# Attention inside a decoder block: two heads' gathers on the two halves of the array's columns, and the running product scanned in place in SBUF

## The reference

```python
def block(args):
    qi, i = args
    logits = jnp.einsum('bqhd,bkhd->bhqk', qi, k, preferred_element_type=jnp.float32) * scale
    mask = key_pos[None, :] < q_pos[:, None]
    log_beta = jax.nn.log_sigmoid(logits)
    log_1m_beta = jnp.where(mask, jax.nn.log_sigmoid(-logits), 0.0)
    after = lax.cumsum(log_1m_beta, axis=3, reverse=True) - log_1m_beta
    w = jnp.where(mask, jnp.exp(log_beta + after), 0.0)
    return jnp.einsum('bhqk,bkhd->bqhd', w.astype(v.dtype), v)
```

## Time and profile before

| | us |
|---|---|
| three runs: median | 2991.63 |
| lowest, highest | 2988.93, 2992.62 |
| the profiled execution: span from its first to its last instruction | 2988.6 |

### The profile page before, as it was taken

How to read it: one execution, slowest core, us unless ns; L and a number is a source line. 1 busy time by engine, 2 the same in 40 slices (tenths; PEclk the granted TensorE clock), 3 DMA queues, 4 the chain that set the end, 5 groups by cost and what they waited for, 6 DMA issues and landing times. The chain is left out here.

```text
span 2988.6 us, 43206 instructions
## 1 busy us (share of the span) xinstructions
PE 2801.2 (94%) x14883; PEld 2366.7 (79%) x14883; DVE 1855.9 (62%) x2803; ACT 1357.4 (45%) x2268; POOL 906.7 (30%) x711
## 2 busy tenths in 40 slices
PE   6999977889999998997899899999999899999998
PEld 5888854779889897885788778887888787878787
DVE  5334348867778786555567675657555748484753
ACT  4222225667767675222344455555555424242421
POOL 0111101645555551310000022223333344434442
PEclk9999988989999999998999999999999999999999
DMA  5433344282322203443123334333544364656554
GB/s 171 104 87 82 98 128 58 71 216 54 71 57 58 61 22 103 136 145 134 57 99 106 120 103 141 110 112 116 182 140 137 103 168 101 170 103 158 113 113 85
DMA packets 291396, 328.21 MB, mean 110 GB/s; under 512 B 114072, under 2 KB 220576, under 8 KB 290976
## 3 DMA queue, kind: packets, MB, share of 16 engines
q1 hardware_dynamic: 276960, 291.96, 32.9%
q0 software_dynamic: 13824, 33.56, 7.5%
q10 hardware_dynamic: 464, 0.79, 0.1%
HBM read 206.57 MB, written 126.88 MB: 112 GB/s over the span
## 5 line engine op out<-in xcount | busy, mean ns | idle before, releaser
L3260 PE MATMUL f_ps_bank<-f_big,h_wv 128*128 128x512 f32 x1280 | 502.6, 393 | 25.3 <-DVE f_big L3106 18.6
L3262 PE MATMUL f_ps_bank<-f_big,h_wv 128*128 128x512 f32 x1280 | 500.1, 391 | 0.0
L3261 PE MATMUL f_ps_bank<-f_big,h_wv 128*128 128x512 f32 x1280 | 500.0, 391 | 0.0
L738 POOL TENSOR_TENSOR a_w<-a_on,a_left 128x640 f32<-128x640 f32 (+5 forms) x192 | 282.4, 1471 | 244.7 <-DVE a_left L790 113.1
L3003 ACT ACTIVATE h_wv<-h_w_sum 128x512 fp32r<-128x512 f32 x252 | 159.0, 631 | 351.1 <-PE f_ps_bank L3262 348.8
L2946 POOL TENSOR_TENSOR h_w_sum<-h_w_raw 128x512 f32<-128x512 f32 x63 | 90.6, 1438 | 730.3 <-DMA h_w_raw<-in_w_up 452.1
L3260 PEld LDWEIGHTS f_ps_bank<-f_big,h_wv 128*128 128x128 f32 x1280 | 241.4, 189 | 82.4 <-issue 27.2
L3262 PEld LDWEIGHTS f_ps_bank<-f_big,h_wv 128*128 128x128 f32 x1280 | 241.4, 189 | 50.6
L3261 PEld LDWEIGHTS f_ps_bank<-f_big,h_wv 128*128 128x128 f32 x1280 | 241.6, 189 | 49.5
L880 PE MATMUL a_ps_y<-a_wt,a_v 128*96 128x128 f32 x2176 | 269.9, 273 | 3.6 <-DVE a_yt L813 2.1
L3102 DVE TENSOR_TENSOR h_wv<-h_w_raw,h_wv 128x512 fp32r<-128x512 f32 x189 | 171.5, 908 | 155.0 <-ACT h_wv L3003 151.6
(11 more groups left out here) (402 smaller groups left out, 6155.7 us busy)
## 6 DMA issues: line engine op xcount, KB each, us to landing
h_w_raw<-in_w_up SPq DMA_DIRECT2D x32, 1024.0 KB, 6.6
a<-h_xr SPq DMA_DIRECT2D x128, 256.0 KB, 3.4
h_w_raw<-a SPq DMA_DIRECT2D x32, 1024.0 KB, 5.2
h_raw<-in_w_down SPq DMA_DIRECT2D x32, 512.0 KB, 6.6
out<-h_xr POOLq DMA_DIRECT2D x64, 256.0 KB, 4.7
out<-h_xr POOLq DMA_DIRECT2D x32, 512.0 KB, 5.6
p_xt<-in_x SPq DMA_DIRECT2D x16, 512.0 KB, 4.5
q<-p_raw SPq DMA_DIRECT2D x64, 128.0 KB, 2.5
```

The lines of the kernel that those rows point to most:

```text
L738: pool.tensor_tensor(w[m % WS][:, 0:k1 - k0], on[m % ONS][:, 0:k1 - k0], left[a][i % 2][:, at + k0 + 1:at + k1 + 1], ALU.mult).then_inc(we ...
L3260: pe.matmul(o, wv(i, 0)[:, k, :], hv(i, 0)[:, k, :], start=(k == 0), stop=False)
L3261: pe.matmul(o, wv(i, 0)[:, k, :], hv(i, 1)[:, k, :], start=False, stop=False)
L3262: mm = pe.matmul(o, wv(i, 1)[:, k, :], hv(i, 0)[:, k, :], start=False, stop=(k == KH - 1))
```

## The change

Two things are changed, both in `stick_breaking`.

The gathers of the two heads of a unit are issued together, tile by tile in turn, head 0 into rows 0 to 63 of the output and head 1 into rows 64 to 127, with 64 columns of v each. A pair is gathered after both its slots, in every second iteration. One semaphore counts pairs. y of both heads is then in one tile, and is copied by one DVE instruction and stored by one DMA.

The second sigmoid is written to `left` in SBUF, and the scan runs over `left` in place. The wait for `left` moves from DVE to ACT, and `score(m)` waits for the second sigmoid of slot m - 2, no more for its scan.

```diff
-        yt = [sb(f"yt{a}", [HEAD, 2, BANK]) for a in range(2)]
+        yt = sb("yt", [P, 2, BANK])
...
+        def wait_gathered(eng, slots):
+            wait(eng, pairs_gathered, (slots + 1) // 2)
...
-                act.activation(z, z, ACT.Sigmoid, scale=-SCALE).then_inc(sig_off, 1)
+                at = SEQ - (i + 1) * P
+                if blocks_of[m] >= 2:
+                    act.wait_ge(weighed, final_slot[blocks_of[m] - 2] + 1)
+                act.activation(left[a][i % 2][:, at + k0:at + k1], z, ACT.Sigmoid, scale=-SCALE).then_inc(sig_off, 1)
...
                 dve.wait_ge(sig_off, m + 1)
-                if blocks_of[m] >= 2:
-
-                    dve.wait_ge(weighed, final_slot[blocks_of[m] - 2] + 1)
                 if not first:
                     dve.wait_ge(scanned, m - 1)
-                dve.tensor_tensor_scan(left[a][i % 2][:, at + k0:at + k1][:, ::-1], z_ps[m % 2][:, 0:k1 - k0][:, ::-1],
+                part = left[a][i % 2][:, at + k0:at + k1][:, ::-1]
+                dve.tensor_tensor_scan(part, part,
                                        one[:, 0:1].to_broadcast([P, k1 - k0]),
...
-                if last:
+                if last and a == 1:
                     part = s * 4 + i // 4
-                    dve.wait_ge(gathered, m + 1)
-                    if part >= 2:
-                        dve.wait_ge(y_stored[part % 2], part // 2 * 2 * DMA)
-                    dve.tensor_copy(yt[a][:, part % 2, i % 4 * P:(i % 4 + 1) * P], y_ps[a][0:HEAD, 0:P]).then_inc(y_copied, 1)
+                    wait_gathered(dve, m + 1)
+                    wait(dve, y_stored[part % 2], part // 2 * DMA)
+                    dve.tensor_copy(yt[:, part % 2, i % 4 * P:(i % 4 + 1) * P], y_ps[blocks_of[m] % 2][:, 0:P]
+                                    ).then_inc(y_copied, 1)
...
                 if m >= 2:
-                    pe.wait_ge(scanned, m - 1)
+                    pe.wait_ge(sig_off, m - 1)
...
-                    cols = slice(row * HEAD, row * HEAD + TALL)
-                    mm = pe.matmul(y_ps[a][0:TALL, 0:P], v[a][(2 * s + half) % 3][:, cols],
-                                   wt[m % WTS][:, t, :], start=(first and t == 0), stop=(last and t == tiles - 1))
-                mm.then_inc(gathered, 1)
+                    cols = slice(row * HEAD, (row + 1) * HEAD)
+                    for a in range(2):
+                        mm = pe.matmul(y_ps[blocks_of[m] % 2][a * HEAD:(a + 1) * HEAD, 0:P], v[a][(2 * s + half) % 3][:, cols],
+                                       wt[(m + a) % WTS][:, t, :], start=(first and t == 0), stop=(last and t == tiles - 1))
+                mm.then_inc(pairs_gathered, 1)
...
-                if m >= GATHER_LAG:
-                    gather(m - GATHER_LAG)
+                if m > GATHER_LAG and m % 2:
+                    gather(m - GATHER_LAG - 1)
```

More of the change, by code:

```diff
@@ L591, in stick_breaking @@
     WIDE = 1024
-    TALL = 3 * HEAD // 2
     UNITS = attention_units()
@@ L607, in stick_breaking @@
         k2_lo = [[sb(f"k2_lo{a}{r}", [P, HALF], F32R) for r in range(3)] for a in range(2)]
-        v = [[sb(f"v{a}{r}", [P, BLOCKS * HEAD // 2 + HEAD // 2]) for r in range(3)] for a in range(2)]
+        v = [[sb(f"v{a}{r}", [P, BLOCKS * HEAD // 2]) for r in range(3)] for a in range(2)]
         ident = sb("ident", [P, P])
@@ L637, in stick_breaking @@
         copied_d = sem("copied_d")
-        gathered = sem("gathered")
+        pairs_gathered = sem("pairs_gathered")
         y_copied = sem("y_copied")
@@ L684, in load_half @@
                                          k_dram[2 * s + a, part * HEAD:(part + 1) * HEAD, cols]).then_inc(k_loaded[half], DMA)
-                wait(sp, gathered, (step_out + 1) * PER_STEP)
+                wait_gathered(sp, (step_out + 1) * PER_STEP)
                 for a in range(2):
                     h = 2 * s + a
-                    sp.dma_start(v[a][r][:, 0:BLOCKS * HEAD // 2].rearrange("p (i d) -> p i d", d=HEAD),
+                    sp.dma_start(v[a][r][:, :].rearrange("p (i d) -> p i d", d=HEAD),
                                  v_dram[cols, h * HEAD:(h + 1) * HEAD].rearrange("(i p) d -> p i d", p=P)).then_inc(v_loaded[half], DMA)
@@ L692, in store_half @@
                 for part in (2 * half, 2 * half + 1):
[L693 to L697, removed]
+                    wait(sp, y_copied, s * BLOCKS + (part + 1) * 4)
+                    sp.dma_start(yt_dram[s * P:(s + 1) * P, part * BANK:(part + 1) * BANK], yt[:, part % 2, :]
+                                 ).then_inc(y_stored[part % 2], DMA)
             load_begin(sp, 0, slice(0, BANK), begin_loaded[0], begin_loaded[0])
             for a in range(2):
-                sp.dma_start(v[a][0][:, 0:BLOCKS * HEAD // 2].rearrange("p (i d) -> p i d", d=HEAD),
+                sp.dma_start(v[a][0][:, :].rearrange("p (i d) -> p i d", d=HEAD),
                              v_dram[0:HALF, a * HEAD:(a + 1) * HEAD].rearrange("(i p) d -> p i d", p=P)
@@ L713, in _ @@
                 else:
-                    sp.wait_ge(y_stored[0], (2 * s + 1) * 2 * DMA)
+                    sp.wait_ge(y_stored[0], (2 * s + 1) * DMA)
                     ahead.load_ys(sp, yt_dram, ahead_loaded)
@@ L718, in _ @@
             for part in range(2):
-                sp.wait_ge(y_stored[part], 2 * STEPS * 2 * DMA)
+                sp.wait_ge(y_stored[part], 2 * STEPS * DMA)
         @block.gpsimd
@@ L758, in copies @@
                         act.wait_ge(turned, g + 1)
-                        if m >= WTS:
-                            act.wait_ge(gathered, m - WTS + 1)
+                        wait_gathered(act, m - WTS + 1)
                         act.activation(wt[m % WTS][:, t0:t0 + n, :], wt_ps[g % 2][:, 0:n * P].rearrange("p (t q) -> p t q", q=P),
@@ L775, in _ @@
             dve.memset(one[:, :], 1.0).then_inc(ones_ready, 1)
[L776 to L779, removed]
+            dve.wait_ge(ones_ready, 5)
             def scan(m):
@@ L799, in copies @@
                         dve.wait_ge(turned, g + 1)
-                        if m >= WTS:
-                            dve.wait_ge(gathered, m - WTS + 1)
+                        wait_gathered(dve, m - WTS + 1)
                         dve.tensor_copy(wt[m % WTS][:, t0:t0 + n, :],
@@ L825, in _ @@
             pe.wait_ge(constants, 5)
-            pe.wait_ge(ones_ready, 11)
             def score(m):
@@ L867, in gather @@
             def gather(m):
-                s, a, i, k0, k1, first, last = SLOTS[m]
-                wait_copied(pe, first_group[m + 1] - 1)
+                s, _, i, k0, k1, first, last = SLOTS[m]
+                wait_copied(pe, first_group[m + 2] - 1)
                 if first:
@@ L873, in gather @@
                         pe.wait_ge(v_loaded[i // (BLOCKS // 2)], (s + 1) * 2 * DMA)
-                    wait(pe, y_copied, 2 * (blocks_of[m] - 1) + a + 1)
+                    wait(pe, y_copied, blocks_of[m] - 1)
                 tiles = (k1 - k0) // P
```

## The result

The changed kernel took 3031.78 us (median of four runs, 3029.23 to 3033.84), the kernel before 2990.28 (2985.85 to 2992.62): ratio 1.0138, 95% interval 1.0124 to 1.0153. Slower by 41 us; 3031 was forecast, range 3011 to 3078.

The account below looks back on a forecast made before the run. PE bounded attention before; now scans and products in turns would: 552 + 7 + 4 = 563 us, plus 4.5 us behind, ending at 1177.5 instead of 1137.66, so 2991.6 + 40 = 3031 us, range 3011 to 3078.

Parts of the forecast that it names:

- The exclusion: In attention, a scan with two SBUF inputs and GpSimd's product cannot overlap; chance 0.78, 3031 us, 3011 to 3078.
- The sum: Attention's scans and products in turns: 552 us lower bound, plus 7 and 4, gives 563 us.
- the queue: Scans and products each waiting behind the other, saving 0.14 us each; five slots in six, the others costing 7 us.
- short slots: Slots starting each of attention's four steps, bound by latency: 4 us added.
- The upper bound: Each product starts 0.08 us after its scan, and the next scan waits for that product: 594 us.
- The tail: From attention's last product to its end: transposes, copies, the last pair's gathers, a copy of y; 4.5 us.
- The gathers: Attention's paired gathers overlap in the array's halves: PE saves 119 us, shape changes add 19, load 416 us.
- Rival 1: Scans and products in attention overlap as before and the array's halves overlap: 2910 us, chance 0.10.
- Rival 2: In attention, scans and products overlap as before but the array's halves don't: 2991 to 3011, say 3002 us, chance 0.04.
- Rival 3: Exclusion, with PE also bounding attention through serial or dearer halves or a falling clock: 3080 to 3100 us, chance 0.08.
- The sigmoid into SBUF: Attention's second sigmoid written to SBUF costs ScalarE 1 us, nothing; z comes free about 1.7 us sooner.
- Copies of y: VectorE loses 64 of attention's 128 copies of y, 17 us less load; the rest fit into GpSimd's turns.

Follow-up runs that it names:

- experiment 1: Kernel before with only the second sigmoid written to left in SBUF and the scan in place there; gathers unchanged: 3041.71 us, ratio 1.0171.
- experiment 5: Changed kernel with the scan's column of ones in a PSUM bank, y in one bank and copied one slot earlier: 2953.41 us, ratio 0.987.
- Experiment 3: Changed kernel with z in PSUM as the scan's ignored second operand, scores waiting for the scan again: 2952.66 us, ratio 0.9875.
- Experiment 10: Changed kernel with each pair's gather cut into two shares, after the odd and the next even slot: 3021.49 us, ratio 1.0102.
- Experiment 4: Changed kernel with VectorE waiting for product m - 1 before scan m: 3123.61 us, ratio 1.0446.
- Experiment 6: Experiment 2 with all of head 0's blocks in a pair first, then all of head 1's: 3029.19 us, ratio 1.0126.
- experiment 7: Kernel before with gathers of 64 columns of v instead of 96, still one head at a time: 3044.81 us, ratio 1.018.
- experiment 2: Changed kernel with the second sigmoid back in PSUM, the scan reading it there, and the waits of before: 2954.97 us, ratio 0.988.
- Experiment 8: Experiment 2 with each pair's gather cut into two shares, a fifth wt buffer, y copied one slot later: 2938.78 us, ratio 0.983.

## Why the prediction was right, and where its steps were off

**The exclusion (right, shown).** Two SBUF inputs, though one is a single repeated column, make scan and product take turns: experiment 1 gets all of the loss without the pairs, and experiment 5 removes it by moving only that column to PSUM (its other edits, one bank for y and an earlier copy of y, touch neither the scan nor the product). Experiment 3 removes it with z in the column's place. The rule that the prediction took from the Trainium skill (SBUF — State Buffer, § SBUF: two separate sides) holds for this operand too; 2.29 became up to 4.02 us.

**The sum (right in size, partly by luck).** From the first scan at 610.55 to the last product's end at 1173.43 it is 562.9 us; 563 were forecast as 552, plus 7 for one slot in six out of the queue, plus 4 for short slots. Two terms were off, in opposite directions. The queue saves more than was taken: a waiting scan saves its 0.14 us (2.29 - 2.14 = 0.15 above), but a waiting product 0.20, not 0.14. With that the bound for a queue that never runs dry is 605.7 - 192 x 0.34 = 540 us, an estimate from these rows, and not 552. Experiment 10 bears this out: it reaches 552.7 although 26 of its products were out of the queue. So what the changed kernel loses outside the queue is about 23 us, not 11. The share of slots was nearly right (38 of 192, one in five), their price was not.

The causes named were incomplete too. I laid the loss to copies between scans and to the latency of short slots. Experiment 10 keeps both, except that y is copied a slot later, and is 10 us shorter: so much came with the length of PE's bursts. In the changed kernel 16 of the 38 late products stand beyond the first 16 slots of a step, in experiment 10 only 2 of 26; what is left, about 13 us, lies mostly in the starts of the four steps. PE, ScalarE and GpSimd of the changed kernel at 652 us, then a window of PE with the granted clock (third figure from the end):

```profile
652.33 1.49 PE L858 MATMUL a_ps_wt<-a_ident,a_w 128*128 128x128 f32 x8 [1.92 <-DVE a_wt L798]
653.75 2.94 PE L876 MATMUL a_ps_y<-a_wt,a_v 128*64 128x128 f32 x28
...
657.74 0.70 ACT L751 ACTIVATE a_on<-a_ps_z 128x640 f32<-128x640 f32 x1 [3.56 <-PE a_ps_z L846]
...
658.43 1.09 POOL L738 TENSOR_TENSOR a_w<-a_on,a_left 128x512 f32<-128x512 f32 x1 [1.75 <-PE a_ps_wt L858]
660.95 1.32 POOL L738 TENSOR_TENSOR a_w<-a_on,a_left 128x640 f32<-128x640 f32 x1 [1.43 <-DVE a_left L787]
663.73 1.32 POOL L738 TENSOR_TENSOR a_w<-a_on,a_left 128x640 f32<-128x640 f32 x1 [1.47 <-DVE a_left L787]
666.48 1.32 POOL L738 TENSOR_TENSOR a_w<-a_on,a_left 128x640 f32<-128x640 f32 x1 [1.43 <-DVE a_left L787]
```

```profile
653.70:656.70 3.00, 3.00 (x30) 2.77 (x29) 1.93 (x2) 0.49 (x1) 2.98 (x2) 0.58 0.00 0
```

PE had waited 1.92 us for VectorE's copy, the granted clock then stood at 0.58 (five sixths of the window at the 1.2 GHz level, one sixth at 2.4), and a burst of 28 took 2.94 us where it takes 1.75 at full clock. The score behind it came 3.56 us late for ScalarE, the queue in front of GpSimd ran dry, and GpSimd then idled 1.43 to 1.47 us ahead of each of four products in a row, until VectorE had its lead back. How much of this is the length of the burst and how much its lower clock is not separated.

**The upper bound (sound for turns without a lead, not reached).** 594 us has each product start 0.08 us after its scan, while the next scan waits at the lock and saves 0.14. The changed kernel shows this state in the rows above: from 663.73 to 666.48 it is 2.75 us a slot, and 1.47 + 1.32 + 0.08 - 0.14 = 2.73. Had it stayed there for all 192 slots, it would have taken about the 594. It did not, since four products in five found their scan done. Experiment 4 is another chain, which the range did not have to hold: where a semaphore orders the turns nothing waits at the lock, so nothing is taken off, 0.10 + 0.08 us are added, and with the starts of the steps it takes 653 us, 90 more than the changed kernel.

**The tail (right).** 5.1 us from the last product to the end, 4.5 forecast; 64 gathers in 3.71 us, 0.055 each. The forecast's terms add up to 3.9 (1.04 + 0.6 + 2.0 + 0.3) and were rounded up to 4.5 without a reason. I had counted the last pair alone, 32 records in 2.0 us; the order on PE puts the pair before it behind the last transposes too, 1.7 us more, which in turn hides the copies (0.6) that I had added.

**The gathers (mechanism right, sizes off).** Halves overlap, at 0.055 us a record: the sentence of the Trainium skill (TensorEngine Tiling (Array Packing), § Tiling Modes) by which column tiles load and multiply independently agrees with 0.055 against 0.113, and the rule (TensorE: Matmul & The Clock Gate, § Part 3) that a load overlaps only in another row group does not fit it. Experiment 6 adds that only records that stand close together overlap. The change of shape is right as well: 0.1 us, 0.11 and 0.09 in experiment 7. What was wrong is the load made of them, 416 us: without the exclusion it is 445 (experiment 2). Part of that is no work at all: the same PE instructions show 445.3, 453.6 and 496.5 us busy in experiment 2, the changed kernel and experiment 4, whose PE stops ever more often; the modelled end of the last record before a stop and the lower clock would both do this, which I have not separated.

**The rivals.** Rival 1 came true in experiments 2, 3 and 5, where the exclusion is away: 2953 to 2955 instead of 2910. Its order was right, its price 43 us too good, because the 15 us that a chain of three nearly full engines was said to lose had no row: the pairs put two heads' gathers in one block (1.75 us for 28 records), in which no score is issued. Experiment 8 gets 16 us of that back although it adds 20 us of PE work. The other 28 stay open. PE is then busy 458.8 us of the 477.5 of its stage and bounds it again, with a load above the 416 of the forecast:

```profile
608.00:1085.50 477.50, 458.76 (x4175) 359.62 (x4174) 388.43 (x370) 371.59 (x614) 281.84 (x192) 0.99 0.31 80
```

Rival 2's premise, that halves don't overlap, fell. Rival 3 did not decide, but its clock did play: 0.96 over the stage, and 0.58 at 653.7. Its price did not follow from its load: 594 us of PE from 609.95 end at 1204, 66 us later than 1137.66, which is 3058 us and not 3080 to 3100.

**The sigmoid into SBUF (right).** Experiments 2 and 3 differ in it and are 2 us apart, which is within the noise. That z comes free sooner is worth nothing measurable (experiment 5). **Copies of y (right).** 16.9 us for 64 instead of 33.5 for 128, and nobody waited for it.

## What to carry to other kernels

Before moving an operand from PSUM to SBUF, count the SBUF inputs of each VectorE instruction that runs beside a GpSimd product on SBUF, repeated columns included: here the second one cost both engines their overlap, and moving back one operand restored it. Where two engines must take turns, keep both queued; an ordering semaphore added 92 us here. Two half-width products for the two halves of the columns paid when they alternated record by record, at a price of 0.1 us at each change of shape. In this kernel short runs of them were better than long ones, since what a burst delayed cost more than the changes it saved.

## What the runs showed of the hardware that was not expected

- A VectorE scan and a GpSimd product exclude each other (both up to 4.0 us) when the scan's second SBUF input is a single repeated column, even one whose value is ignored; with that column in PSUM (experiment 5), or z in its place (experiment 3), the scan keeps 2.35 us at most and the product 2.01.
- What had waited at the lock saved part of its length: a scan 0.15 us (2.14 for 2.29), a product 0.20 (1.57 for 1.77).
- Half-width products in one half take 0.113 us a record, slightly more than 96 rows (0.109); alternating halves 0.055. Where all of one head's records come before the other's, a few still overlap at the seam (28 in 2.89 us, 3.21 if none did).
- With 1.92 us of waiting ahead of it PE ran at a granted clock of 0.58 for 3 us. In experiment 4, where PE waits in every slot, the stage's mean was 0.89:

```profile
608.00:1269.00 661.00, 496.52 (x4176) 406.48 (x4176) 391.38 (x370) 369.74 (x614) 282.08 (x192) 0.89 0.22 58
```
